# Scan's filler products cut into pieces of two contraction tiles, two of them moved between the six mask products

## The chip, the cores and the metric

The kernel runs on one core of one Trainium2 chip. The metric is the device time of one execution in microseconds (us); lower is better. Engines are called PE (TensorE matmul), PEld (TensorE weight load), DVE (VectorE), ACT (ScalarE), POOL (GpSimd) and SP (SyncE, which issues the DMAs).

## The reference, cut to what matters

Two layers of a backbone over 512 latent tokens and 256 context tokens. Each layer projects the modulated input `h` by one wide weight `w_in` (queries, keys, values, Fourier channels, gates, recurrent channels), runs three branches on parts of that projection, merges them, and ends in a convolutional feed-forward block. One branch is a bidirectional recurrence (8 heads of 64 channels, two directions); the first layer needs its outputs for all tokens, the last layer for the context tokens needs the final state alone.

```python
def _in_proj(h, w_in, names=None):
    out, off = {}, 0
    for name, width in IN_GROUPS:
        if names is None or name in names:
            out[name] = h @ w_in[:, off:off + width]
        off += width
    return out

def _wkv_scan(decay, kd, v, kk, b, s0, r=None):
    ...
    def step(s, inp):
        w_t, k_t, v_t, kk_t, b_t = inp[:5]
        sk = jnp.einsum('dbhvk,dbhk->dbhv', s, kk_t)
        s = s * w_t[..., None, :] - sk[..., None] * b_t[..., None, :] + v_t[..., None] * k_t[..., None, :]
        y = jnp.einsum('dbhvk,dbhk->dbhv', s, inp[5]) if len(inp) == 6 else None
        return s, y
```

## The kernel before, in words

The change lies in `rwkv_scan`, which runs once per layer. It computes the recurrence in blocks: a group `g` is 128 tokens of each direction `d` (two chunks of 64), and a layer has six groups, two of context tokens and four of latent ones. A group is a chain of small steps, PE product, then DVE or ACT on the result, then the next PE product. While PE would wait for the other engines it works on something else: the products of the wide input projection that the recurrence does not need (value, query, key, Fourier and gate channels). These are the filler products, issued by `fill(point, g)` (matmuls of L893).

The work of `fill` is planned ahead. There are 52 slots (128 output channels each, one 512 KB weight block); a slot is one piece for the 512 latent tokens and, where context tokens are needed too, one for the 256 context tokens. A piece is eight contraction tiles of 128 (`KT` = 8), accumulated in one PSUM bank, and each contraction tile is three fp32r matmuls (high and low halves of the operands): 512 or 256 columns wide. Pieces are cut into parts (L736): before, a 512-wide piece is two parts of four contraction tiles, a 256-wide piece is one part of eight, so a part is 12 matmuls 512 wide or 24 matmuls 256 wide. The list `wanted` says at which point of a group a part stands, in the order in which points get their share, and `points` is the order in which they come in the program. Each finished piece is copied from PSUM by ACT (L1119), split and stored; ACT walks the same points in `copy_pieces`.

The first step of a direction is the one that the change touches. PE computes four or six masked products, 16 matmuls of 64x64 each (L916), in this order: NAT and T (banks 0 and 1), MT and, where outputs are wanted, QB (banks 2 and 3), then QK where outputs are wanted and TT (banks 4 and 5). DVE multiplies each by a mask on its way to SBUF (L1267 NAT, L1268 T, L1270 MT, L1272 QB, L1274 QK, L1276 TT). DVE starts NAT when the second product is done, MT when the fourth is done and QK when the last is done. PE then transposes four operands (L937) into banks 0 to 3, and for that waits until all masks are done (semaphore `prod`), since the banks are reused. Before, `fill("prod0" or "prod1", g)` stands between the last product and the transposes, with one part. Behind the transposes stands `fill("turn0" or "turn1", g)`, which has a part in the first layer and none in the last. The second direction's products first wait for ACT's copies of the first one's transposes. Then come five levels of a triangular inverse for both directions (L945 to L1002, L1291 to L1305), and the state steps (L1015 to L1100), each with its fill points.

In the first layer all six groups want outputs: 12 directions of six products. In the last layer the two context groups don't: 4 directions of four products and 8 of six. A direction is named below by the time at which its first product starts.

Of the kernel before, what the change touches and what calls it, by code (L numbers as in the profile page):

```python
# [32 lines left out]
KT = D_MODEL // P  # L33
# [101 lines left out]
def program(nc, A, out):  # L135
    with ExitStack() as top:
# [314 lines left out]
        BOTH = ((0, SEQ), (SEQ, CTX_LEN))  # L451
# [235 lines left out]
        def rwkv_scan(l, s2, h, rings, o_w, last, late):  # L687
# [13 lines left out]
            Kttm, NAT, T, TT, Y, MT = ([spare[:, (2 * i + d) * GCOL:(2 * i + d + 1) * GCOL] for d in range(2)] for i in range(6))  # L701
# [31 lines left out]
            ends = [sum(p <= s for p, _ in pieces) for s in range(len(slots))]  # L733
            parts = []
            for i, (s, w) in enumerate(pieces):
                parts += [(i, s, w, range(0, 4)), (i, s, w, range(4, 8))] if w == BOTH[0] else [(i, s, w, range(8))]  # L736

            points = ["prod0", "turn0", "prod1", "turn1"] + [f"{k}{n}" for n in range(5) for k in ("Y", "offT")]
            points += ["W1", "W2", "U0", "S0", "U1", "S1", "end"]
            wanted = ["prod0", "prod1", "W1", "W2", "U0", "S0", "U1", "S1"] + [f"Y{n}" for n in range(5)] + [f"offT{n}" for n in range(5)]  # L740
            wanted += ["end", "turn1", "turn0"] + [f"offT{n}" for n in range(5)] + ["W1", "prod0", "prod1"]
            n_first = 8
            share = [(len(parts) - n_first) * (g + 1) // N_G - (len(parts) - n_first) * g // N_G for g in range(N_G)]
            span, first = {("first", 0): (0, n_first)}, n_first
            for g in range(N_G):
# [23 lines left out]
            with stage(nc) as (block, sem):  # L769
# [109 lines left out]
                def _(pe):  # L879
# [19 lines left out]
                    for g in range(N_G):  # L899
                        want_y, R = want[g], rI[g % 2]  # L900
                        for d in range(2):

                            pe.wait_ge(sem("fm"), before(n_fm, g, d) + n_fm[g])
                            if d:
                                pe.wait_ge(sem("tm"), 8 * g + 4)
                            elif g:
                                pe.wait_ge(sem("S"), 2 * g)
                                if want[g - 1]:
                                    pe.wait_ge(sem("YR"), y_before(g))
                                    pe.wait_ge(sem("Ysum"), y_before(g))  # L910

                            def product(b, o, stat, mov, turned_rows=False):
                                for t in range(CTILES):
                                    for i in range(2):
                                        for hh in range(2):
                                            m = pe.matmul(ps[rows(row_of(hh, t, i) if turned_rows else i), (b + hh) * 512 + o + t * C:(b + hh) * 512 + o + (t + 1) * C],  # L916
                                                          stat[rows(hh), tc(t, i):tc(t, i) + C], mov[rows(hh), tc(t, i):tc(t, i) + C],
                                                          start=True, stop=True)
                                m.then_inc(sem("pmm"), 1)

                            product(0, 0, Bh[d], Kt[d], True)
                            product(0, 256, Kt[d], Bh[d], True)
                            product(2, 0, EN[d], Kt[d])
                            if want_y:
                                product(2, 256, Bh[d], R[d])
                            if d:
                                pe.wait_ge(sem("prod"), before(n_pr, g, d))
                            if want_y:
                                product(4, 0, EN[d], R[d])
                            product(4, 256, Bh[d], Kt[d])  # L930
                            fill(f"prod{d}", g)

                            pe.wait_ge(sem(f"v{d}"), 16 * (g + 1))
                            pe.wait_ge(sem("prod"), before(n_pr, g, d) + n_pr[g])
                            for b, src in ((0, Kt[d]), (1, Bp[d]), (2, Lr[d]), (3, vI[d])):
                                for t in range(CTILES):
                                    m = pe.transpose(bank(b, P, t * P), src[:, t * P:(t + 1) * P], ident[:, :])  # L937
                                m.then_inc(sem("tmm"), 1)
                            fill(f"turn{d}", g)
# [168 lines left out]
                def _(act):  # L1108
# [44 lines left out]
                        act.wait_ge(sem("exp"), n + 3)  # L1153
                        act.activation(L[:, :], L[:, :], ACT.Exp, scale=-DECAY).then_inc(sem("exp"), 1)

                    copy_pieces(0, "first", some=slice(0, 2))
                    decays(0, 0)
                    copy_pieces(0, "first", some=slice(2, 6))
                    decays(0, 1)
                    copy_pieces(0, "first", some=slice(6, n_first))  # L1160
                    for g in range(N_G):
                        for d in range(2):
                            for n_tm, (b, dst) in enumerate(((0, Kttm), (1, Btm), (2, Ktm), (3, Vtm))):
                                act.wait_ge(sem("tmm"), 8 * g + 4 * d + n_tm + 1)
                                act.activation(dst[d][:, :], bank(b), ACT.Copy).then_inc(sem("tm"), 1)
                            copy_pieces(g, f"prod{d}", f"turn{d}")
                        for n_lv in range(5):
                            for d in range(2):
                                act.wait_ge(sem(f"Ymm{d}"), 5 * g + n_lv + 1)
# [1344 lines left out]
```

## Time and profile before

| | |
|---|---|
| runs of the kernel before, median of 3 | 3658.41 us (3656.13 to 3660.78) |
| span of the profiled execution | 3653.4 us, 5.0 us below that median |
| PE busy | 3375.0 us (92%) |
| PEld busy | 2696.8 us (74%) |
| DVE busy | 1582.8 us (43%) |
| ACT, POOL busy | 1268.5 us (35%), 1071.4 us (29%) |
| PE matmul and weight-load instructions | 36725 each |
| mean granted TensorE clock | 0.971 |
| scan of the first layer, of the last layer | about 255 to 880 us, about 2270 to 2800 us |

Times in rows count from the span's start. The span is from the first to the last instruction of one execution; a run's time holds it and what lies around it, so the times of the runs are a few us longer.

### The profile page before, as it was taken

The page shows a single profiled execution, that of the slowest core. Times are in us where ns is not written, and L with a number is a line of the kernel's source. Part 1 is how long each engine was busy: PE and PEld are TensorE (multiplying, and loading weights), DVE is VectorE, ACT ScalarE, POOL GpSimd, SP SyncE. Part 2 cuts the span into 40 slices and gives each one's busy share as a digit, 9 for nine tenths or more (in the row PEclk, how much of TensorE's full clock was granted, in tenths as well). Part 3 has the DMA queues.
Part 4 walks back from the last instruction along what each step waited for, and adds up shares of the span by engine and source line. Part 5 has one row for each costly group of instructions (what it writes and reads, how often), then busy time and mean ns, then how long its engine had stood idle before and what let it go on. Part 6 is the DMA issues. An engine that isn't in the chain of part 4 may idle for free. (4 is left out here: it accounts for less than half of the span.)

```text
span 3653.4 us, 82760 instructions
## 1 busy us (share of the span) xinstructions
PE 3375.0 (92%) x36725; PEld 2696.8 (74%) x36725; DVE 1582.8 (43%) x2538; ACT 1268.5 (35%) x2184; POOL 1071.4 (29%) x645
## 2 busy tenths in 40 slices
PE   6989999999888999799999899999899898889998
PEld 4668888888655777687878676887778666568887
DVE  3243334442377546512112734445453476372224
ACT  3333233333365412321212243334344465233222
POOL 1111133233011412332333132223333114235553
PEclk8999999999999999999999999999999999989999
DMA  7664333443212343233332145344343313423332
GB/s 260 213 204 113 111 113 90 119 121 96 83 58 96 102 140 104 81 116 121 116 116 94 50 142 182 101 113 128 115 128 92 104 58 121 165 84 104 98 98 87
DMA packets 444861, 423.43 MB, mean 116 GB/s; under 512 B 15652, under 2 KB 372042, under 8 KB 437594
## 3 DMA queue, kind: packets, MB, share of 16 engines
q1 hardware_dynamic: 442922, 409.35, 35.7%
q10 hardware_dynamic: 1584, 8.78, 0.6%
q8 instruction: 291, 4.77, 0.5%
q14 instruction: 64, 0.52, 0.0%
HBM read 329.34 MB, written 88.74 MB: 114 GB/s over the span
## 5 line engine op out<-in xcount | busy, mean ns | idle before, releaser
L893 PE MATMUL ps<-I-321_h_hi,I-324_w_hi 128*128 128x256 f32 (+1 forms) x832 | 294.8, 354 | 4.5 <-PEq L124 4.5
L893 PE MATMUL ps<-I-322_h_lo,I-324_w_hi 128*128 128x256 f32 (+1 forms) x832 | 282.0, 339 | 0.0
L893 PE MATMUL ps<-I-321_h_hi,I-325_w_lo 128*128 128x256 f32 (+1 forms) x832 | 281.8, 339 | 0.0
L2372 POOL TENSOR_TENSOR I-18800_w_lo<-I-18798_w_raw,I-18799_w_hi 128x1024 fp32r<-128x1024 f32 x60 | 145.1, 2418 | 342.6 <-ACT I-18799_w_hi L2335 342.5
L893 PE MATMUL ps<-I-23550_h_hi,I-23553_w_hi 128*128 128x512 f32 (+1 forms) x544 | 212.7, 391 | 4.6 <-PEq L124 4.6
L893 PE MATMUL ps<-I-23551_h_lo,I-23553_w_hi 128*128 128x512 f32 (+1 forms) x544 | 200.9, 369 | 0.0
L893 PE MATMUL ps<-I-23550_h_hi,I-23554_w_lo 128*128 128x512 f32 (+1 forms) x544 | 200.6, 369 | 0.0
L2372 POOL TENSOR_TENSOR I-39040_w_lo<-I-39038_w_raw,I-39039_w_hi 128x1024 fp32r<-128x1024 f32 x60 | 144.5, 2408 | 154.6 <-ACT I-39039_w_hi L2335 154.6
L2335 ACT ACTIVATE I-18799_w_hi<-I-18798_w_raw 128x1024 fp32r<-128x1024 f32 x61 | 64.6, 1059 | 355.0 <-PE ps L370 235.3
L370 PE MATMUL ps<-I-18795_h_hi,I-18799_w_hi 128*128 128x512 f32 x704 | 182.8, 341 | 1.1 <-DVE I-18796_h_lo L407 1.1
L370 PE MATMUL ps<-I-18795_h_hi,I-18800_w_lo 128*128 128x512 f32 x704 | 182.6, 340 | 0.0
L370 PE MATMUL ps<-I-18796_h_lo,I-18799_w_hi 128*128 128x512 f32 x704 | 180.1, 337 | 0.0
L893 PEld LDWEIGHTS ps<-I-321_h_hi,I-324_w_hi 128*128 128x128 f32 x832 | 158.5, 191 | 25.4 <-issue 4.9
L857 POOL TENSOR_TENSOR I-325_w_lo<-I-323_w_raw,I-324_w_hi 128x1024 fp32r<-128x1024 f32 x34 | 81.9, 2408 | 320.1 <-ACT I-324_w_hi L1137 320.1
L893 PEld LDWEIGHTS ps<-I-321_h_hi,I-325_w_lo 128*128 128x128 f32 x832 | 158.5, 191 | 17.2
L893 PEld LDWEIGHTS ps<-I-322_h_lo,I-324_w_hi 128*128 128x128 f32 x832 | 158.8, 191 | 14.6
L1119 ACT ACTIVATE I-1999_result<-ps 128x512 f32<-128x512 f32 x104 | 51.3, 493 | 327.7 <-PE ps L893 327.5
L857 POOL TENSOR_TENSOR I-23554_w_lo<-I-23552_w_raw,I-23553_w_hi 128x1024 fp32r<-128x1024 f32 x34 | 83.7, 2462 | 275.7 <-ACT I-23553_w_hi L1137 275.7
L963 PE MATMUL ps<-I-49_x 64*64 64x32 f32 x3840 | 149.3, 220 | 1.4 <-issue 1.4
L370 PE MATMUL ps<-I-39035_h_hi,I-39039_w_hi 128*128 128x512 f32 x352 | 137.9, 392 | 1.1 <-DVE I-39036_h_lo L407 1.1
L370 PE MATMUL ps<-I-39036_h_lo,I-39039_w_hi 128*128 128x512 f32 x352 | 137.1, 389 | 0.0
L370 PE MATMUL ps<-I-39035_h_hi,I-39040_w_lo 128*128 128x512 f32 x352 | 137.0, 389 | 0.0
(902 smaller groups left out, 8757.7 us busy)
## 6 DMA issues: line engine op xcount, KB each, us to landing
I-323_w_raw<-in_w_in SPq DMA_DIRECT2D x67, 512.0 KB, 5.8
I-23552_w_raw<-in_w_in SPq DMA_DIRECT2D x67, 512.0 KB, 5.2
I-18808_ada_w<-in_ada_w SPq DMA_DIRECT2D x24, 1024.0 KB, 6.0
I-18798_w_raw<-in_ffn_up SPq DMA_DIRECT2D x44, 512.0 KB, 3.8
I-39038_w_raw<-in_ffn_up SPq DMA_DIRECT2D x44, 512.0 KB, 3.8
proj_d<-I-1999_result SPq DMA_DIRECT2D x52, 384.0 KB, 3.0
I-507_ada_w<-in_ada_w SPq DMA_DIRECT2D x16, 1024.0 KB, 5.8
I-18798_w_raw<-in_ffn_down SPq DMA_DIRECT2D x22, 512.0 KB, 3.3
```

Of the source, the lines that this page charges most:

```text
L370: m = pe.matmul(dst[:, at:at + n], w[wi][:, k, :], a[ai][:, k, at:at + n], start=k == 0 and i == 0, stop=k == kt - 1 and i == 2)
L857: pool.tensor_tensor(lo(s), raw(s), hi(s).bitcast(F32), ALU.subtract).then_inc(sem("w_lo"), 1)
L893: m = pe.matmul(bank(6 + i % 2, n_c), w[:, k, :], hv[:, k, c0:c0 + n_c], start=k == 0 and v == 0, stop=k == KT - 1 and v == 2)
L963: return pe.matmul(side(ps[rows(i), (2 + d) * 512 + c0:(2 + d) * 512 + c0 + C], n_lv, 1 - d), Y[d][rows(i), c0:c0 + C], side(TT[d][rows(i) ...
L1119: act.activation(res[:, s % 2, c0:c0 + n_c], bank(6 + i % 2, n_c), ACT.Copy, scale=DH_A ** -0.5 if J_Q <= slots[s][0] < J_K else 1.0).then ...
L2335: act.activation(pair(g)[0], rings[0][:, g % 3, :, :], ACT.Copy).then_inc(sem("w_hi"), 1)
L2372: pool.tensor_tensor(pair(g)[1], rings[0][:, g % 3, :, :], pair(g)[0].bitcast(F32), ALU.subtract).then_inc(sem("w_lo"), 1)
```

## The change

A part is halved: two contraction tiles of a 512-wide piece, four of a 256-wide one (6 or 12 matmuls). The number of parts doubles, every entry of `wanted` stands twice, and the first 16 half parts instead of the first 8 parts stand ahead of the first group. In place of one part at `prod0` and `prod1`, one half part stands at a new point, `early0` or `early1`, behind the second product, and one at `prod0` or `prod1`, behind the fourth where outputs are wanted; where they are not, that half part stays behind the last product. ACT's copies follow the same points.

```diff
-                parts += [(i, s, w, range(0, 4)), (i, s, w, range(4, 8))] if w == BOTH[0] else [(i, s, w, range(8))]
-
-            points = ["prod0", "turn0", "prod1", "turn1"] + [f"{k}{n}" for n in range(5) for k in ("Y", "offT")]
+                n_k = 2 if w == BOTH[0] else 4
+                parts += [(i, s, w, range(k, k + n_k)) for k in range(0, KT, n_k)]
+
+            points = ["early0", "prod0", "turn0", "early1", "prod1", "turn1"] + [f"{k}{n}" for n in range(5) for k in ("Y", "offT")]
...
-            n_first = 8
+            whole = ["W1", "W2", "U0", "S0", "U1", "S1"] + [f"Y{n}" for n in range(5)] + [f"offT{n}" for n in range(5)]
+            whole += ["end", "turn1", "turn0"] + [f"offT{n}" for n in range(5)] + ["W1", "prod0", "prod1"]
+            wanted = ["early0", "prod0", "early1", "prod1"] + [p for p in whole for _ in range(2)]
+            n_first = 16
...
                             product(0, 0, Bh[d], Kt[d], True)
                             product(0, 256, Kt[d], Bh[d], True)
+                            fill(f"early{d}", g)
                             product(2, 0, EN[d], Kt[d])
                             if want_y:
                                 product(2, 256, Bh[d], R[d])
+                                fill(f"prod{d}", g)
                             if d:
                                 pe.wait_ge(sem("prod"), before(n_pr, g, d))
                             if want_y:
                                 product(4, 0, EN[d], R[d])
                             product(4, 256, Bh[d], Kt[d])
-                            fill(f"prod{d}", g)
+                            if not want_y:
+                                fill(f"prod{d}", g)
```

On PE, the first direction of the last group of the last layer before (the first row is the last filler matmul ahead of it; `kk_in` and `EN` hold scaled keys, `Bh` and `r_in` the other operands, `ident` is the identity of the transposes; the filler rows left out repeat the three shown):

```order
L893 MATMUL ps<-I-23550_h_hi,I-23554_w_lo 128x512
L916 MATMUL ps<-I-24941_kk_in,I-24931_Bh 64x64 x16
L916 MATMUL ps<-I-24931_Bh,I-24941_kk_in 64x64 x16
L916 MATMUL ps<-I-24941_kk_in,I-24927_EN 64x64 x16
L916 MATMUL ps<-I-24945_r_in,I-24931_Bh 64x64 x16
L916 MATMUL ps<-I-24945_r_in,I-24927_EN 64x64 x16
L916 MATMUL ps<-I-24941_kk_in,I-24931_Bh 64x64 x16
L893 MATMUL ps<-I-23550_h_hi,I-23553_w_hi 128x512
L893 MATMUL ps<-I-23551_h_lo,I-23553_w_hi 128x512
L893 MATMUL ps<-I-23550_h_hi,I-23554_w_lo 128x512
...
L937 MATMUL ps<-I-50_ident,I-24941_kk_in 128x128 x4
```

The same place on PE after the change, with the new line numbers:

```order
L918 MATMUL ps<-I-24941_kk_in,I-24931_Bh 64x64 x16
L918 MATMUL ps<-I-24931_Bh,I-24941_kk_in 64x64 x16
L895 MATMUL ps<-I-23550_h_hi,I-23553_w_hi 128x512
...
L918 MATMUL ps<-I-24941_kk_in,I-24927_EN 64x64 x16
L918 MATMUL ps<-I-24945_r_in,I-24931_Bh 64x64 x16
L895 MATMUL ps<-I-23550_h_hi,I-23553_w_hi 128x512
...
L918 MATMUL ps<-I-24945_r_in,I-24927_EN 64x64 x16
L918 MATMUL ps<-I-24941_kk_in,I-24931_Bh 64x64 x16
L942 MATMUL ps<-I-50_ident,I-24941_kk_in 128x128 x4
```

The twelve filler matmuls that stood between the sixth product and the transposes stand in two lots of six, behind the second and the fourth product, and the transposes follow the sixth product directly.

On PE, the first direction of the last layer's first context group before, four products and 24 filler matmuls 256 wide, and then after the change:

```order
L916 MATMUL ps<-I-24941_kk_in,I-24931_Bh 64x64 x16
L916 MATMUL ps<-I-24931_Bh,I-24941_kk_in 64x64 x16
L916 MATMUL ps<-I-24941_kk_in,I-24927_EN 64x64 x16
L916 MATMUL ps<-I-24941_kk_in,I-24931_Bh 64x64 x16
L893 MATMUL ps<-I-23550_h_hi,I-23553_w_hi 128x256
...
L937 MATMUL ps<-I-50_ident,I-24941_kk_in 128x128 x4
```

```order
L918 MATMUL ps<-I-24941_kk_in,I-24931_Bh 64x64 x16
L918 MATMUL ps<-I-24931_Bh,I-24941_kk_in 64x64 x16
L895 MATMUL ps<-I-23550_h_hi,I-23553_w_hi 128x256
...
L918 MATMUL ps<-I-24941_kk_in,I-24927_EN 64x64 x16
L918 MATMUL ps<-I-24941_kk_in,I-24931_Bh 64x64 x16
L895 MATMUL ps<-I-23550_h_hi,I-23553_w_hi 128x256
...
L942 MATMUL ps<-I-50_ident,I-24941_kk_in 128x128 x4
```

Here half of the filler matmuls, twelve, moved ahead of the third product, and twelve stay ahead of the transposes. On ACT, DVE, POOL and SP no instruction changes its place. Over a group the number of filler matmuls is the same to within one half part.

## Rows read from the trace of the kernel before

**Rows 1.** PE's waits (line waited for: us in total, times, longest us), first layer's scan.

```profile
PE ps L916 <- issue: 18.2, 12, 3.4
PE ps L1068 <- DVE I-49_x L1339: 6.7, 3, 4.8
```

**Rows 2.** The same view, last layer's scan.

```profile
PE ps L916 <- issue: 8.6, 6, 1.8
PE ps L958 <- DVE I-49_x L1291: 6.3, 4, 4.3
```

**Rows 3.** Timeline (start us, us, engine line op) of the direction that starts at 730.46.

```profile
730.14 0.39 PE L893 MATMUL ps<-I-321_h_hi,I-325_w_lo 128*128 128x512 f32 x1
730.46 0.69 PE L916 MATMUL ps<-I-1991_kk_in,I-1981_Bh 64*64 64x64 f32 x32
...
730.95 1.29 POOL L866 TENSOR_TENSOR I-1999_result<-I-1999_result,I-2000_rope 128x512 f32<-128x512 f32 x1
...
731.69 0.69 DVE L1267 TENSOR_TENSOR I-49_x<-ps,I-1954_masks 128x512 f32<-128x512 f32 x1 [3.35 <-PE ps L916]
...
734.29 0.45 PE L916 MATMUL ps<-I-1991_kk_in,I-1981_Bh 64*64 64x64 f32 x14 [0.93 <-issue]
...
734.67 0.50 PE L893 MATMUL ps<-I-321_h_hi,I-324_w_hi 128*128 128x512 f32 x1
...
734.79 0.69 DVE L1274 TENSOR_TENSOR I-1971_QK<-ps,I-1954_masks 128x512 f32<-128x512 f32 x1 [0.62 <-PE ps L916]
735.01 0.39 PE L893 MATMUL ps<-I-322_h_lo,I-324_w_hi 128*128 128x512 f32 x1
...
735.40 0.68 DVE L1276 TENSOR_TENSOR I-49_x<-ps,I-1954_masks 128x512 f32<-128x512 f32 x1
...
737.53 0.60 PE L937 MATMUL ps<-I-50_ident,I-1991_kk_in 128*128 128x128 f32 x4
```

**Rows 4.** DMA queues (packets, MB, share of 16 engines): whole span, then 731.8 to 732.9.

```profile
q8 instruction: 291, 4.77, 0.5%
...
q8 instruction: 1, 0.02, 5.6%
```

**Rows 5.** Windows (columns in the first row), first product to first transpose, 19 directions.

```profile
core 0: us, PE busy (x) PEld busy (x) DVE busy (x) ACT busy (x) POOL busy (x), PEclk, DMA share, GB/s
...
391.19:402.34 11.15, 7.74 (x205) 6.54 (x205) 5.07 (x8) 0.00 (x0) 1.85 (x1) 0.85 0.38 106
...
2473.37:2479.30 5.93, 5.93 (x216) 5.86 (x217) 4.67 (x8) 2.70 (x5) 0.00 (x0) 1.00 0.01 3
...
2769.91:2775.74 5.83, 5.83 (x205) 5.21 (x205) 4.56 (x8) 0.00 (x0) 0.00 (x0) 1.00 0.02 5
...
sum 147.06, PE 121.24 PEld 107.85 DVE 97.37 ACT 25.95 POOL 50.25; mean PE 6.38 PEld 5.68 DVE 5.12 ACT 1.37 POOL 2.64
```

**Rows 6.** Timeline of the first direction of the first layer, its last mask and transposes.

```profile
273.40 0.68 DVE L1276 TENSOR_TENSOR I-49_x<-ps,I-1954_masks 128x512 f32<-128x512 f32 x1
...
274.23 0.63 PE L937 MATMUL ps<-I-50_ident,I-1991_kk_in 128*128 128x128 f32 x4 [1.33 <-DVE I-49_x L1276]
```

**Rows 7.** Windows: stretches in and behind idle stretches of PE, columns as in rows 5.

```profile
281.63:283.63 2.00, 0.01 (x1) 0.00 (x0) 0.93 (x2) 0.00 (x0) 0.00 (x0) 1.00 0.00 0
858.83:861.98 3.15, 0.00 (x1) 0.00 (x0) 0.69 (x2) 0.00 (x0) 2.79 (x3) 1.00 0.42 120
862.60:866.00 3.40, 3.40 (x10) 2.63 (x9) 2.33 (x4) 0.00 (x0) 0.00 (x0) 0.50 0.00 0
...
2566.34:2568.07 1.73, 0.00 (x0) 0.00 (x0) 0.69 (x2) 1.30 (x3) 0.27 (x1) 1.00 0.18 46
2569.20:2572.60 3.40, 3.40 (x9) 2.55 (x9) 3.33 (x3) 0.00 (x0) 3.40 (x3) 0.50 0.22 65
...
276.30:279.70 3.40, 3.40 (x68) 2.67 (x70) 0.00 (x0) 1.87 (x4) 1.38 (x1) 1.00 0.46 127
```

**Rows 8.** DMA queues, 856.7 to 859.4 us.

```profile
q1 hardware_dynamic: 1439, 0.72, 99.9%
```

More of the change, by code:

```diff
@@ L735, in rwkv_scan @@
             for i, (s, w) in enumerate(pieces):
-                parts += [(i, s, w, range(0, 4)), (i, s, w, range(4, 8))] if w == BOTH[0] else [(i, s, w, range(8))]
-            points = ["prod0", "turn0", "prod1", "turn1"] + [f"{k}{n}" for n in range(5) for k in ("Y", "offT")]
+                n_k = 2 if w == BOTH[0] else 4
+                parts += [(i, s, w, range(k, k + n_k)) for k in range(0, KT, n_k)]
+            points = ["early0", "prod0", "turn0", "early1", "prod1", "turn1"] + [f"{k}{n}" for n in range(5) for k in ("Y", "offT")]
             points += ["W1", "W2", "U0", "S0", "U1", "S1", "end"]
-            wanted = ["prod0", "prod1", "W1", "W2", "U0", "S0", "U1", "S1"] + [f"Y{n}" for n in range(5)] + [f"offT{n}" for n in range(5)]
-            wanted += ["end", "turn1", "turn0"] + [f"offT{n}" for n in range(5)] + ["W1", "prod0", "prod1"]
-            n_first = 8
+            whole = ["W1", "W2", "U0", "S0", "U1", "S1"] + [f"Y{n}" for n in range(5)] + [f"offT{n}" for n in range(5)]
+            whole += ["end", "turn1", "turn0"] + [f"offT{n}" for n in range(5)] + ["W1", "prod0", "prod1"]
+            wanted = ["early0", "prod0", "early1", "prod1"] + [p for p in whole for _ in range(2)]
+            n_first = 16
             share = [(len(parts) - n_first) * (g + 1) // N_G - (len(parts) - n_first) * g // N_G for g in range(N_G)]
@@ L1154, in decays @@
                         act.activation(L[:, :], L[:, :], ACT.Exp, scale=-DECAY).then_inc(sem("exp"), 1)
-                    copy_pieces(0, "first", some=slice(0, 2))
+                    copy_pieces(0, "first", some=slice(0, 4))
                     decays(0, 0)
-                    copy_pieces(0, "first", some=slice(2, 6))
+                    copy_pieces(0, "first", some=slice(4, 12))
                     decays(0, 1)
-                    copy_pieces(0, "first", some=slice(6, n_first))
+                    copy_pieces(0, "first", some=slice(12, n_first))
                     for g in range(N_G):
@@ L1165, in _ @@
                                 act.activation(dst[d][:, :], bank(b), ACT.Copy).then_inc(sem("tm"), 1)
-                            copy_pieces(g, f"prod{d}", f"turn{d}")
+                            copy_pieces(g, f"early{d}", f"prod{d}", f"turn{d}")
                         for n_lv in range(5):
```

## Prediction

> **What bounds the kernel now.** I read the waits of PE first, since PE is busy for 92% of the span. In the scans the largest entry is "L916 <- issue", 18.2 us in 12 waits in the first layer and 8.6 us in 6 in the last [rows 1, 2]: "issue" means that PE waits for nothing that another engine does. The timeline of one direction shows where. PE runs through five masked products and half of the sixth without a break, stands for 0.93 us with 14 of the sixth's 32 rows to go, and goes on [rows 3]. The DMA view has an instruction queue that carries 291 packets, 4.77 MB; with 73,450 matmuls and weight loads on PE in the table above that is one packet of 16 KB for about 256 PE instructions, and in this direction one of them stands alone in the window ahead of the break [rows 4]. I read the break as PE out of instructions: six products are 384 of them (192 matmul rows, 192 loads) and pass in 2.8 us, faster than the next packet comes. The windows view then prices it. From first product to first transpose a direction takes 5.83 us without a break (a 256-wide filler part: 5.93 us), and up to 11.15 us with one; 19 of the 20 six-product directions together take 147.06 us [rows 5]. The reader is to see that this stretch is a pure PE chain: DVE and ACT are waited for nowhere in it. The twentieth is the very first direction, where DVE is late and ends the wait [rows 6].
>
> The second thing in these windows is the clock. Behind a break of 3.15 us and behind one of 1.73 us the granted clock is 0.50, the 1.2 GHz level, for about 3.4 us; in a break of 2.00 us, and in the window of the direction that holds it, it is 1.00 [rows 7].
>
> **What the change removes.** The base without breaks is 15 x 5.83 + 4 x 5.93 = 111.2 us, so breaks and slow clock cost 147.06 - 111.2 = 35.9 us in these 19 directions. With filler matmuls behind the second and the fourth product, the 256 records between two packets no longer pass in 1.9 us. The break with 14 rows to go puts the packet boundary ahead of it into the second product (192 - 14 = 178 rows, with the loads 356 instructions, less 256: the 100th, and a product has 64); to the next boundary PE then has two lots of fillers, about 2 x 1.3 us, and most of the four other products, together about 4.5 to 5 us. From a boundary to the resumption it takes the 1.9 us that 256 product instructions need, plus the break: 1.9 + 0.93 + 0.22 = 3.1 us in the direction shown, and some 5.3 us where data traffic holds the packet up (the break of 3.15 us, with the data queue at 99.9% just before it, [rows 7, 8]). So I take all of the 35.9 us as saved, less 0.7 us that the two late packets may still cost.
>
> **What it adds.** All new durations are in one direction's rows [rows 3]. The first filler matmul starts 0.15 us behind the last product matmul (which starts at 734.29 + 0.45 - 0.22 = 734.52), the second 0.34 us behind the first, the others 0.229 us apart (735.01 to 737.53 is 11 steps), and from the last filler matmul to a product it is 0.32 us (730.14 to 730.46). Half a part is 0.34 + 4 x 0.229 = 1.26 us from first to last. The six products alone are 5.83 - 2.86 - 0.15 = 2.82 us, in three pairs 2.79 us. So from first product to last product matmul: 2.79 + 2 x (0.15 + 1.26 + 0.32) = 6.25 us.
>
> Then comes the wait that the filler part used to hide. QK and TT can be masked only when the last product is done, and the transposes wait for TT. QK starts 734.79 - 734.52 = 0.27 us behind the last product matmul, TT 0.61 us later [rows 3], and the transposes 0.83 us behind TT's start (273.40 to 274.23, [rows 6]): 1.71 us with no cover. In the kernel before the same 1.71 us lay under 2.86 us of filler. A direction becomes 6.25 + 1.71 = 7.96 us, 2.13 us over the unbroken 5.83 us; a 256-wide one shifts by the same. 19 x 2.13 = 40.5 us.
>
> The bounds of the 1.71 us: not under 1.4 us (two masks at 0.60 us and the two hand-overs cannot overlap), and not much over it, unless POOL slows the masks; with POOL busy beside it (730.95 to 732.24) the mask at 731.69 took 0.69 us as elsewhere [rows 3], so I take 1.71. What is queued behind the waiting transposes on PE is the turn filler, the second direction and the five levels; nobody else waits meanwhile, since ACT only copies transposes.
>
> The four-product directions had no break and keep half a part ahead of the transposes, 1.6 us, which hides the one late mask. They pay the extra switch alone: 0.15 + 0.32 us, less 0.11 us as one filler step falls away, 0.35 us each, 1.4 us in all. The first direction of all stays bound by DVE: zero. The doubled lists move filler work by at most half a part at other points and cost nothing where the pieces end as before; no other engine's order changes.
>
> **The sum.** -35.9 + 0.7 + 40.5 + 1.4 = +6.7 us: 3653.4 + 6.7 = 3660.1 us of span. The runs' median lies 5.0 us over the span, so 3665 us, +0.18%. In words: the break in the instruction stream goes, and a wait for DVE of the same size takes its place.
>
> The Trainium skill's page "Runtime: NRT & Kernel Launch", section "Instruction fetch mechanics", describes the refills in blocks of 256 instructions and says of a crossing that it is "mostly hidden". The trace disagrees for these products: 18 breaks, 26.8 us together [rows 1, 2]. By the page nothing would be saved and the sum would be near +42 us, which is the first rival.
>
> **Rivals.** First, slower: the breaks stay, because a packet is asked for only after PE has gone some way into the block and the wait for DVE then holds up the asking. For it: the packet came some 2 us later where data traffic was thick [rows 8]. Against it: the boundary falls into the second product, and 2.6 us of filler now lie behind it. If all stayed, the 35.9 us would not be saved: about 3700 us. From a fifth of them on (7 us) it decides between no difference and slower.
>
> Second, slower: the clock. Each direction now has PE idle for about 1.5 us (1.71 less the last matmul's 0.22) with only short matmuls and transposes around it. A break of 1.73 us was followed by the lower level, one of 2.00 us shows no such thing [rows 7]. A slow stretch of 3.4 us at half speed costs at most 1.7 us; I take 1.5 us each time. If a third of 19 waits do it, +9.5 us, 3674.5 us; all of them, 3693 us. The Trainium skill's page "TensorE: Matmul & The Clock Gate", Part 4, says that transposes do not count as PE being busy; by that the idle stretch would be longer than the 1.5 us and the falls likely. The trace does not bear it out: behind the first direction's wait of 1.33 us [rows 6] and its transposes the window from 276.30 us shows the granted clock at 1.00 [rows 7].
>
> Third, faster: the waits for DVE elsewhere, 6.7 us at the state step [rows 1] and 6.3 us at the levels [rows 2], with one slow-clock stretch behind each of the longest two. DVE is late there with preparing the next group, whose loads and POOL's splits follow the filler pieces. Where the filler stream is shifted by half a part, these start about 1.4 us earlier. If all vanished: 13 us and some 6 us of clock, 3665 - 19 = 3646 us. It decides when 14 of the 19 us go. Against it: one part more or less early is 1.4 us, and the two longest waits are 4.8 and 4.3 us.
>
> That the change doesn't do what it says is excluded: the new order has the fillers between the products.
>
> **How the numbers follow.** A difference under 0.2%, 7.3 us, can't be told from none in this kernel. My forecast has a chance of 0.66, with 3658 to 3673 us as its own range; the clock 0.18, the breaks 0.07, the faster waits 0.09. The predicted time is the forecast's. The range of 8 in 10 takes in the clock's third and leaves its far end and the breaks: 3656 to 3678 us. Faster by over 0.2%: 0.08, from the third rival. Slower by over 0.2%: most of the first two (0.21) and a third of the forecast (0.21), 0.42. Same: 0.50.
>
> **What would show it.** In the new profile the waits "L918 <- issue" should fall from 26.8 us to a few us, and a wait of the transposes for DVE's TT (L942) should appear, about 1.5 us each, some 28 us in about 20 waits. The windows from first product to first transpose should all be near 8.0 us. The half-clock stretches behind the products, at 863 and 2569 us in the old trace, should be gone. I am wrong if the transposes' wait is much shorter than 1.5 us, if issue waits stay above 10 us, or if the lower clock level appears behind the new waits.

## The result and the profile after

The changed kernel takes 3668.53 us (median of 10 runs, 3662.38 to 3676.89), the kernel before took 3655.75 us beside it (10 runs, 3651.27 to 3664.23). The ratio is 1.0035, with a 95% interval of 1.0024 to 1.0046: slower by some 13 us, and more than the 0.2% that can be told from none. The forecast was 3665 us.

PE's waits in the first layer's scan come first, as in [rows 1] (line waited for: us in total, times, longest us). In the changed kernel the products are at L918, the fillers at L895, the transposes at L942. The view begins at 160 us; its entries for PEq and ada_row lie ahead of the scan.

```profile
PE ps L942 <- DVE I-49_x L1281: 18.0, 12, 1.5
PE ps L1073 <- DVE I-49_x L1344: 5.7, 3, 4.8
PE ps L895 <- PEq L124: 4.5, 1, 4.5
PE ps L198 <- ACT I-66_ada_row L189: 2.5, 1, 2.5
PE ps L895 <- ACT I-2001_turned L1131: 2.4, 1, 2.4
PE ps L963 <- DVE I-49_x L1296: 0.2, 1, 0.2
```

The same view of the last layer's scan, against [rows 2]:

```profile
PE ps L942 <- DVE I-49_x L1281: 12.0, 8, 1.5
PE ps L963 <- DVE I-49_x L1296: 6.5, 3, 4.3
...
PE ps L968 <- DVE I-49_x L1296: 1.8, 1, 1.8
```

"L918 <- issue" is in neither list: all 26.8 us of breaks in the instruction stream are gone. In their place stand 20 waits of the transposes for DVE, 30.0 us. The waits for DVE at the state step (9.4 us over both scans in either kernel) and at the levels (7.2 against 6.9 us) are nearly what they were. Two entries are new that I had not forecast: fillers that wait for ACT's rotated copies (2.4 us), and a level step that waits 1.8 us for DVE.

The timeline shows one six-product direction as it now runs (one of the kernel before stands in [rows 3]): two products, half a part, two products, half a part, two products, then an empty PE.

```profile
631.97 0.65 PE L918 MATMUL ps<-I-1982_Bh,I-1992_kk_in 64*64 64x64 f32 x32
...
632.55 0.50 PE L895 MATMUL ps<-I-321_h_hi,I-324_w_hi 128*128 128x512 f32 x1
...
637.33 0.65 PE L918 MATMUL ps<-I-1992_kk_in,I-1982_Bh 64*64 64x64 f32 x32
...
638.04 0.69 DVE L1279 TENSOR_TENSOR I-1972_QK<-ps,I-1954_masks 128x512 f32<-128x512 f32 x1 [1.39 <-PE ps L918]
638.65 0.68 DVE L1281 TENSOR_TENSOR I-49_x<-ps,I-1954_masks 128x512 f32<-128x512 f32 x1
...
639.48 0.63 PE L942 MATMUL ps<-I-50_ident,I-1992_kk_in 128*128 128x128 f32 x4 [1.50 <-DVE I-49_x L1281]
```

The windows from first product to first transpose of the same 19 directions as in [rows 5], and the two stretches behind such a wait:

```profile
core 0: us, PE busy (x) PEld busy (x) DVE busy (x) ACT busy (x) POOL busy (x), PEclk, DMA share, GB/s
394.95:403.01 8.06, 6.56 (x211) 5.63 (x211) 3.97 (x7) 0.00 (x0) 1.83 (x1) 1.00 0.54 148
...
2482.42:2490.51 8.09, 6.59 (x216) 6.08 (x217) 3.97 (x7) 2.71 (x5) 0.00 (x0) 1.00 0.02 4
...
2787.25:2795.28 8.03, 6.53 (x206) 5.20 (x205) 3.98 (x7) 0.00 (x0) 0.00 (x0) 1.00 0.01 2
...
sum 152.99, PE 124.48 PEld 102.96 DVE 75.53 ACT 22.48 POOL 52.00; mean PE 6.55 PEld 5.42 DVE 3.98 ACT 1.18 POOL 2.74
```

```profile
639.48:642.90 3.42, 3.42 (x24) 3.12 (x25) 1.71 (x2) 2.07 (x4) 0.56 (x1) 1.00 0.02 7
...
2479.55:2482.95 3.40, 2.46 (x50) 2.26 (x54) 1.27 (x2) 2.71 (x6) 0.12 (x1) 1.00 0.00 0
```

The reader is to see that the spread is gone. Before, a direction took anything from 5.83 to 11.15 us; now 18 of the 19 take 8.02 to 8.09 us and one takes 8.25. The sum rises by 152.99 - 147.06 = 5.9 us. The four-product directions take 0.35 to 0.42 us more each, 1.5 us in all, and the first direction 0.7 us less: +6.8 us with rounding. In both stretches behind a wait the clock is at 1.00. In the two scans of this trace it falls four times, each time in or right behind a longer wait (4.8, 2.4, 4.3 and 1.8 us), and never behind one of the 20 waits of 1.5 us.

That is half of the 13 us. Two places in the same scans, outside the first steps, cost another 3.9 and 4.8 us, so 15.5 us are named. The traces scatter by more than what this is off: the span of this one is 21.5 us longer than the one before (3675.0 against 3653.4 us), that of a second trace of the change (below) 9.1 us, with 15.8 us in the same items. So the three items stand in both traces, but how they divide the median's 13 us is not shown.

The first place is in the first layer's fifth group. From the first direction's transposes to the second direction's first product it takes 8.61 us (741.44 to 750.05) against 4.71 before. The timeline of the changed kernel there, then a window (columns as above):

```profile
744.03 0.63 ACT L1124 ACTIVATE I-1999_result<-ps 128x512 f32<-128x512 f32 x1
...
744.68 2.39 ACT L1131 ACTIVATE I-2001_turned<-ps 32x512 f32<-32x512 f32 x4
747.10 0.38 ACT L1124 ACTIVATE I-1999_result<-ps 128x256 f32<-128x256 f32 x1
747.22 0.77 PE L895 MATMUL ps<-I-321_h_hi,I-324_w_hi 128*128 128x512 f32 x1 [2.42 <-ACT I-2001_turned L1131]
```

```profile
746.80:750.20 3.40, 2.98 (x10) 2.00 (x14) 0.00 (x0) 1.69 (x4) 1.54 (x2) 0.50 0.55 202
```

A half part here begins a new piece, in the bank of the piece before the last. ACT empties that bank in five instructions, and only after four copies for the transposes. Of the 3.9 us, 2.4 are the wait; the rest comes with the clock, which is at 0.50, the lower level, behind it.

The second place is in the last layer's fifth group, from the second direction's transposes to the next group: 87.67 against 82.89 us, with 6.8 us at half clock (2747.0 to 2753.8). The two windows, before and after:

```profile
2687.02:2769.91 82.89, 80.84 (x1717) 67.57 (x1716) 36.34 (x70) 35.43 (x77) 32.64 (x20) 1.00 0.49 145
...
2699.58:2787.25 87.67, 82.40 (x1710) 68.77 (x1710) 43.22 (x72) 36.00 (x77) 32.74 (x20) 0.96 0.48 137
```

PE stands idle for 5.3 us in place of 2.1, 3.2 us more, and is busy for 1.6 us more, although half a part less of filler (six matmuls, some 1.4 us) falls into the stretch. So the slow clock costs about 3 us there.

### The profile page after: what moved, and what is told of

It is laid out like the page before. It is cut to its first block and busy times, and to the rows that moved or that the text cites. A ratio compares the mean times of both kernels' runs of the same rounds, so it can differ in the third digit from the quotient of the medians.

```text
span 3675.0 us, 82760 instructions
## 1 busy us (share of the span) xinstructions
PE 3392.7 (92%) x36725; PEld 2700.1 (73%) x36725; DVE 1589.3 (43%) x2538; ACT 1270.0 (35%) x2184; POOL 1068.3 (29%) x645
## 5 line engine op out<-in xcount | busy, mean ns | idle before, releaser
L895 PE MATMUL ps<-I-321_h_hi,I-324_w_hi 128*128 128x256 f32 (+1 forms) x832 | 296.3, 356 | 7.0 <-PEq L124 4.5
L895 PE MATMUL ps<-I-322_h_lo,I-324_w_hi 128*128 128x256 f32 (+1 forms) x832 | 281.8, 339 | 0.0
L895 PE MATMUL ps<-I-321_h_hi,I-325_w_lo 128*128 128x256 f32 (+1 forms) x832 | 281.6, 338 | 0.0
L895 PE MATMUL ps<-I-23550_h_hi,I-23553_w_hi 128*128 128x512 f32 (+1 forms) x544 | 214.2, 394 | 4.6 <-PEq L124 4.6
L895 PE MATMUL ps<-I-23551_h_lo,I-23553_w_hi 128*128 128x512 f32 (+1 forms) x544 | 200.9, 369 | 0.0
L895 PE MATMUL ps<-I-23550_h_hi,I-23554_w_lo 128*128 128x512 f32 (+1 forms) x544 | 200.8, 369 | 0.0
L895 PEld LDWEIGHTS ps<-I-321_h_hi,I-324_w_hi 128*128 128x128 f32 x832 | 158.2, 190 | 28.8 <-issue 8.0
L895 PEld LDWEIGHTS ps<-I-321_h_hi,I-325_w_lo 128*128 128x128 f32 x832 | 158.3, 190 | 17.5
L895 PEld LDWEIGHTS ps<-I-322_h_lo,I-324_w_hi 128*128 128x128 f32 x832 | 158.7, 191 | 14.1
L968 PEld LDWEIGHTS ps<-I-49_x 64*64 64x64 f32 x3840 | 132.4, 136 | 6.7 <-issue 6.4
```

The lines of the kernel that those rows point to most:

```text
L895: m = pe.matmul(bank(6 + i % 2, n_c), w[:, k, :], hv[:, k, c0:c0 + n_c], start=k == 0 and v == 0, stop=k == KT - 1 and v == 2)
L968: return pe.matmul(side(ps[rows(i), (2 + d) * 512 + c0:(2 + d) * 512 + c0 + C], n_lv, 1 - d), Y[d][rows(i), c0:c0 + C], side(TT[d][rows(i) ...
```

## The experiments

In all of them "one half early" means a six-product direction with one half part among its products and the other behind the last.

**The halves back behind the last product.** Parts halved as in the change, both half parts behind the last product.

```diff
-                            fill(f"early{d}", g)
                             product(2, 0, EN[d], Kt[d])
...
                             product(4, 256, Bh[d], Kt[d])
+                            fill(f"early{d}", g)
+                            fill(f"prod{d}", g)
```

> The parts are halved as in the change, but both halves of a direction stay behind its last product. Theory (the breaks in the instruction stream depend on the six products running in one piece; a separate cost of some 4 to 8 us comes from groups that get an odd number of half parts): the breaks return, some 20 to 30 us of issue waits, first product to first transpose is as before, and only the shift costs: about 3656 + 6 = 3662 us, ratio 1.001 to 1.002. Rival (halving costs nothing, the whole 12.8 us are the new place of the fillers): ratio 1.000. Rival (halving alone makes the breaks go): no issue waits at this line, and a gain near 30 us.

Ratio 1.0006 (0.9992 to 1.0020). "L918 <- issue" is back, 19.7 us in the first layer and 8.3 us in the last. Halving alone removes no break; the new places do. A cost of the odd groups is within this interval, but not shown by it. Both places are in its trace: at the first it has the same wait of 2.4 us for ACT's rotated copies, but no slow clock, 7.28 us in place of 4.71; at the second it takes 4.8 us more than before.

**Even groups.** The changed kernel, but each group is given an even number of half parts, so that outside the first steps every point holds what it held before.

```diff
-share = [(len(parts) - n_first) * (g + 1) // N_G - (len(parts) - n_first) * g // N_G for g in range(N_G)]
+share = [2 * ((len(parts) - n_first) // 2 * (g + 1) // N_G - (len(parts) - n_first) // 2 * g // N_G) for g in range(N_G)]
```

> The changed kernel, but each group is given an even number of half parts, so that outside the first steps every filler point holds what it held before. Theory (two costs: about 6.8 us from the first steps, the rest from the odd shift): the filler's wait for ACT's rotated copies behind the transposes goes, and the time is 3656 + 7 = 3663 us, ratio 1.0015 to 1.0025. Rival (the rest is not the shift, but the new place of the first steps' fillers, or chance): ratio stays at 1.0035.

Ratio 1.0018 (1.0006 to 1.0029), 6.6 us; in its trace the first steps cost 6.5 us. All 20 waits of 1.5 us are there, the wait for the rotated copies is gone, and the first place takes 4.74 us again. The second still takes 2.4 us more than before, with the clock at 1.00. The intervals of this ratio and of the change's overlap a little: the trace settles the 3.9 us of the first place, not the rest.

**The changed kernel again**, for a second trace.

> The changed kernel once more, for a second trace. The two places outside the first steps where it lost time, +3.9 us behind the first direction of the first layer's fifth group and +4.8 us behind the last layer's fifth group, the second with a half-clock stretch of 6.8 us. Theory: the first one comes back, since its wait for the rotated copies is set by the order of the parts; the second may not, since a kernel with the same odd groups showed 1.2 us there and one with even groups 5.1 us. Rival (both belong to the odd shift): both come back.

Both places come back, +3.90 and +4.72 us; the run took 3664.45 us. So neither is chance. But the second is in the trace of every kernel with halved parts, from +1.2 to +4.8 us with odd groups and from +2.4 to +5.1 us with even ones, so it is not the odd shift that sets it; the kernels with whole parts and moved packet borders have -0.6 to +1.8 us there. The timeline of this second trace shows DVE's preparation of the next group beside POOL's work:

```profile
2728.84 1.30 POOL L868 TENSOR_TENSOR I-24949_result<-I-24949_result,I-24950_rope 128x512 f32<-128x512 f32 x1 [2.46 <-DMA proj_d<-I-24949_result]
...
2730.21 1.63 POOL L871 TENSOR_TENSOR I-24951_turned<-I-24951_turned,I-24949_result 128x512 f32<-128x512 f32 x1
2730.60 1.78 DVE L1239 TENSOR_TENSOR I-24931_Bh<-I-24929_a,I-24927_EN 128x512 f32<-128x512 f32 x1
2732.27 2.38 POOL L859 TENSOR_TENSOR I-23554_w_lo<-I-23552_w_raw,I-23553_w_hi 128x1024 fp32r<-128x1024 f32 x1 [0.42 <-ACT I-23553_w_hi L1142]
2732.31 2.88 DVE L1241 TENSOR_TENSOR I-24927_EN<-I-24937_k_in,I-24927_EN 128x512 f32<-128x512 f32 x1
2735.12 0.68 DVE L1243 TENSOR_TENSOR I-24933_Bp<-I-24929_a,I-24925_Lr 128x512 f32<-128x512 f32 x1
```

The same chain in the kernel before, five steps of 0.68 us first, then:

```profile
2727.61 1.77 DVE L1244 TENSOR_TENSOR I-24929_a<-I-24945_r_in,I-24937_k_in 128x512 f32<-128x512 f32 x1
2729.42 1.66 DVE L1246 TENSOR_TENSOR I-24945_r_in<-I-24945_r_in,I-24935_L 128x512 f32<-128x512 f32 x1
```

A step of 0.68 us takes 1.7 to 2.9 us where POOL works beside it. Before, two of POOL's three operations fell on the end of the chain and the third behind it; now all three fall on its first three steps. The chain takes 8.2 us in place of 6.5, the level's copies (L1296) come late, and PE stands. In the changed kernel with even groups all three fall on its last steps, and it takes 8.7 us. POOL's chain follows a store's landing (the first row of the second trace names the DMA of `proj_d`), DVE's follows PE's levels; I read it as their phase that decides which of them meet; no run moved the one against the other alone. The Trainium skill's page "SBUF — State Buffer", section "SBUF: two separate sides", says that a DVE operation with two SBUF inputs and a GpSimd operation that reads SBUF exclude each other for a whole instruction. The trace agrees: these steps stretch, while the masks, which read PSUM, keep their 0.69 us beside POOL (638.04 above, with POOL busy for 1.50 of the window's 1.58 us).

**One half early, behind the second product**, with the change's odd groups, then with even groups.

```diff
                             product(0, 256, Kt[d], Bh[d], True)
                             fill(f"early{d}", g)
...
                             product(4, 256, Bh[d], Kt[d])
-                            if not want_y:
-                                fill(f"prod{d}", g)
+                            fill(f"prod{d}", g)
```

> The changed kernel, but in six-product directions too only the first half part stands early, behind the second product, and the second half stays behind the last product. Theory (breaks go once 256 product instructions take over some 3.2 us; the wait for DVE costs only where no filler covers it): a direction takes about 2.8 + 1.73 + 1.71 = 6.25 us, few breaks remain, the transposes' wait for DVE falls from 1.5 us to some 0.1 us each. 19 directions at 0.4 us over the unbroken 5.83 us are +7.8 us, against 35.9 us saved: with the odd shift some 3656 - 28 + 6 = 3634 us, ratio 0.992 to 0.996. Rival (one half part is too little, the next packet is still late): issue waits of 10 us and more behind the products, ratio 0.998 to 1.003. Rival (the clock falls behind any such change): windows at 0.50 behind the products.

> Both edits: one half part early, one behind the last product, and an even number of half parts for each group. Theory: the gains add, about 3656 - 28 + 1 = 3629 us, ratio 0.990 to 0.994, that is some 6 us under the kernel with one early half alone. Rival (the odd shift costs nothing): the same time as that kernel. Rival (the breaks return with one half part): ratio 0.997 to 1.002.

Ratios 0.9961 (0.9947 to 0.9975) and 0.9952 (0.9935 to 0.9968): both faster than before, by 14 and 18 us. In sign the theory holds, a third of the gain is missing. The two intervals overlap, so the 6 us that I expected between these kernels are not shown. Undisturbed directions take 6.55 us, not 6.25, and breaks of 2.3 and 3.6 us remain in the first layer. The timeline of one direction of the kernel with even groups (transposes at L940):

```profile
725.54 0.65 PE L918 MATMUL ps<-I-1993_r_in,I-1977_EN 64*64 64x64 f32 x32
725.79 0.69 DVE L1273 TENSOR_TENSOR I-49_x<-ps,I-1954_masks 128x512 f32<-128x512 f32 x1 [1.39 <-PE ps L918]
726.01 0.65 PE L918 MATMUL ps<-I-1991_kk_in,I-1981_Bh 64*64 64x64 f32 x32
726.40 0.68 DVE L1275 TENSOR_TENSOR I-1969_QB<-ps,I-1954_masks 128x512 f32<-128x512 f32 x1
...
727.00 0.68 DVE L1277 TENSOR_TENSOR I-1971_QK<-ps,I-1954_masks 128x512 f32<-128x512 f32 x1
...
727.60 0.68 DVE L1279 TENSOR_TENSOR I-49_x<-ps,I-1954_masks 128x512 f32<-128x512 f32 x1
...
728.42 0.41 PE L940 MATMUL ps<-I-50_ident,I-1991_kk_in 128*128 128x128 f32 x2 [0.18 <-DVE I-49_x L1279]
```

Four masks run in one chain, 0.61 us apart, from the end of the fourth product; TT is late by that chain, not by the sixth product.

**One half early, behind the fourth product**, even groups.

```diff
-                            fill(f"early{d}", g)
...
                                 product(2, 256, Bh[d], R[d])
+                            fill(f"early{d}", g)
```

> As the kernel with one early half part and even groups, but the early half stands behind the fourth product instead of the second. In that kernel an unbroken direction took 6.55 us, 0.29 us more than the six products, the two half parts and the 1.71 us wait give, because DVE masks four pairs in a chain that starts only after the fourth product. Theory: with the half part behind the fourth product two of the four masks run beside it, QK can start right behind the sixth product, and a direction takes 6.26 us: some 14 x 0.29 = 4 us less than with the half behind the second, ratio to before 0.992 to 0.996. Rival (the first four products in one piece outrun the instruction packets again): breaks of over 10 us in the issue waits, ratio 0.996 to 0.999. Rival (the 0.29 us are not DVE's chain): same time as with the half behind the second.

Ratio 0.9951 (0.9937 to 0.9965): the same as behind the second. An undisturbed direction does take 6.28 us, so the chain of masks was the 0.27 us. But the 19 directions together gain only 1.1 us by it (128.4 against 129.5 us). Nine of them are undisturbed, against twelve with the half behind the second product; the breaks at the products are 3.4 us in the first layer (3.6 there) and 2.4 us in the last (1.0 there).

**The whole part behind the fourth product**, even groups: the change without its split.

> The changed kernel with even groups, but both half parts of a six-product direction stand together behind the fourth product. Theory: one switch between products and fillers less than in the change (0.15 + 0.32 us, less 0.11 us), the same bare wait for DVE: a direction takes 8.02 - 0.36 = 7.66 us, 20 of them some 7 us less than the even version of the change, about 3656 to 3659 us, ratio 0.999 to 1.001, if no breaks return; the transposes' wait stays 1.5 us each. Rival (the first four products run into the packets' end): breaks of 5 to 15 us more. Rival (the added time is not the bare wait but the splitting): a gain of 20 us and more.

Ratio 1.0008 (0.9997 to 1.0020). An undisturbed direction takes 7.64 us, 0.38 less than in the change, with 20 waits for DVE (18.5 us in the first layer, below, and 12.0 in the last) and one break of 0.6 us at the products.

```profile
PE ps L943 <- DVE I-49_x L1282: 18.5, 12, 2.0
```

So the second switch costs 0.38 us a direction, and the bare wait is the main price.

**Packet borders moved.** The kernel before, with 32 small matmul calls ahead of each scan. Each call is two matmul rows and two loads in the trace, so each lot is 128 instructions, not the 64 that I had counted.

```diff
+                    for _ in range(32):
+                        pe.matmul(ps[0:C, 0:C], ident[0:C, 0:C], ident[0:C, 0:C], start=True, stop=True)
                     fill("first", 0)
```

> The kernel before with 32 small matmuls (32 rows and their 32 weight loads, 64 instructions) ahead of each scan; their results are overwritten. Theory (the breaks stand where a packet of 256 PE instructions ends): the breaks of the first layer move by 32 matmul rows, from 14 rows to go in the sixth product to 46 rows to go, that is into the fifth product (or the directions that had none get one); the total of the issue waits may change, the time within 10 us. Rival (the breaks have to do with the place in the direction, a bank, a semaphore or a load, not with the count of instructions): the breaks stay at 14 rows to go.

Ratio 0.9979 (0.9968 to 0.9990). In the first layer, 128 instructions on, the waits at L918 fall from 18.2 to 0.3 us. In the last layer, 256 instructions on, 9.9 us remain, at the rows where they stood before. That is what a border every 256 instructions, 128 rows, would do: in the direction of [rows 3], PE runs from a border at row 50 to one at row 178 in 1.9 us; with the border at row 114 alone, fillers lie ahead of it. The 12 windows of the first layer lose 23.9 us. The window of the fourth direction, 11.15 us in [rows 5], and PE's waits at the products, first layer, then last:

```profile
392.60:398.42 5.82, 5.82 (x206) 5.20 (x206) 4.56 (x8) 0.00 (x0) 1.85 (x1) 1.00 0.73 203
```

```profile
PE ps L918 <- issue: 0.3, 1, 0.3
...
PE ps L918 <- issue: 9.9, 7, 2.1
```

Yet only 8 us are left of it: the added rows made the scan start 5.6 us late, and between the scans, where the borders had moved as well, the trace is 7.3 us longer. That the moved borders cost these 7.3 us is not shown: PE has no wait "<- issue" between the scans in either trace, and the kernel with half the shift (below), whose borders there are moved by the same 128 instructions, is 1.7 us longer than before.

**Borders moved in the first layer only**, 32 narrow calls, put back ahead of its last transposes; then the same with one half early in the last layer.

```diff
+                    for _ in range(0 if last else 32):
+                        pe.matmul(ps[0:C, 0:4], ident[0:C, 0:C], ident[0:C, 0:4], start=True, stop=True)
                     fill("first", 0)
...
                             pe.wait_ge(sem("prod"), before(n_pr, g, d) + n_pr[g])
+                            for _ in range(32 if not last and g == N_G - 1 and d else 0):
+                                pe.matmul(ps[0:C, 0:4], ident[0:C, 0:C], ident[0:C, 0:4], start=True, stop=True)
```

> The kernel before, its own fillers and order, with 32 narrow matmul calls (64 matmul rows and 64 loads, 128 instructions) ahead of the first layer's scan and again ahead of its very last transposes, so that every other stage keeps its packet borders; their results are overwritten. Theory (a direction breaks when two packet borders, 128 rows apart, both fall into its 192 product rows; 128 instructions move them from rows 50 and 178 to row 114 alone): no breaks in the first layer's directions, the last layer's at the same rows as before. The first shifted kernel won 24 us in these windows, lost 5.6 us to wide pads and some 7 us between the scans, where its borders had moved too; here only about 2 us of pads remain: 3657 - 22 = 3635 us, ratio 0.993 to 0.996. Rival (what the breaks cost is lost elsewhere as soon as they go): ratio 0.997 to 0.999, as the first shifted kernel's.

> The same pads, and in the last layer the six-product directions with one half part behind the second product and one behind the last; halved parts, even groups. Theory: on top of the aligned kernel the last layer's directions save about 5 us as in the kernel with one half early: ratio 0.991 to 0.995. Rival (halved parts move DVE's preparation against POOL's work in the last layer, a loss of 3 to 5 us behind its fifth group): no faster than the aligned kernel.

Ratios 0.9963 (0.9951 to 0.9976) and 0.9950 (0.9934 to 0.9965). At the products of the first layer 0.3 us of breaks are left at most, but the pads, as I call the added rows, cost much of what the breaks gave back. The two intervals overlap: a further gain from the half part early in the last layer is not shown by these times. The scan starts 9.3 us late:

```profile
243.20 3.97 PE L899 MATMUL ps<-I-50_ident 64*64 64x4 f32 x36 [4.54 <-PEq L124]
...
854.19 3.89 PE L938 MATMUL ps<-I-50_ident 64*64 64x4 f32 x64
```

```profile
234.70:255.20 20.50, 15.96 (x84) 12.81 (x85) 6.26 (x11) 0.00 (x0) 0.52 (x1) 0.50 0.73 214
```

Rows of 4 columns on one and the same quarter of the array take 0.11 us each at the lower clock and 0.06 at the higher (first fence, timeline). That is no less than the first shift's rows of 64 columns, which took 7.1 us for 64 at the lower clock. The half-clock stretch about the start of the scan is 20.5 us long (second fence, a window), 6.8 to 13.7 us in all the other traces.

**Half that shift**: the first of these two with 16 calls, 64 instructions.

> As the aligned kernel, but with 16 calls instead of 32, 64 instructions. Theory (borders of 256 instructions): the first layer's borders move by 32 rows, from rows 50 and 178 of a direction to about 18 and 146, so the breaks come back, each 32 rows earlier than in the kernel before (143, 145, 132, 156 instead of 175, 177, 164, 188), with issue waits near 18 us in the first layer. Rival (any shift breaks the pattern): no breaks, or breaks at unchanged rows.

One run, 3649.64 us. The breaks come back where the count puts them: in the ninth direction with 14 rows to go in the fifth product, not in the sixth [rows 3]. So do all six breaks of over 0.2 us in the first layer: each stands 32 rows earlier than in the kernel before.

```profile
726.93 0.52 PE L918 MATMUL ps<-I-1993_r_in,I-1977_EN 64*64 64x64 f32 x18
728.08 0.40 PE L918 MATMUL ps<-I-1993_r_in,I-1977_EN 64*64 64x64 f32 x12 [0.63 <-issue]
```

The total is smaller than I expected, 7.7 us against some 18. The first border now lies nearer to the fillers; that the fetch runs ahead of PE there would explain it, but no run tests this.

**Pads moved**: the shift by 128 with one half early in the last layer, its first pads behind the first direction's masks, 32 columns wide and in the products' own order, which alternates between quarters.

```diff
+                            for n in range(32 if not last and (g, d) in ((0, 0), (N_G - 1, 1)) else 0):
+                                i, hh = n // 2 % 2, n % 2
+                                pe.matmul(ps[rows(i), hh * 512:hh * 512 + 32], ident[rows(hh), 0:C], ident[rows(hh), 0:32], start=True, stop=True)
```

> As the aligned mix, but the first pads stand ahead of the transposes of the very first direction, which is not bound by PE's products, instead of ahead of the scan, and both pads are 32 calls of the products' own form, which alternate between the halves of the array. In the aligned kernels the pads ran 0.11 us a row ahead of the scan, on a stretch of half clock that grew from 6.8 to 20.5 us, and made it start 9.3 us late; at the end they took 3.9 us. Theory: at the products' 15 ns a row both pads cost some 1 us each, the breaks stay away, and the time is the aligned mix's less 9.3 - 1 and 3.9 - 1 us: about 3660 - 18 - 11 = 3631 us, ratio 0.990 to 0.993. Rival (the late start of the scan was not the pads' doing): the same ratio as the aligned mix, 0.995.

Ratio 0.9930 (0.9916 to 0.9944), 3633.57 us: 24 us under the kernel before. The pads cost 1.1 and 1.2 us (timeline of the first); place and form of the pads changed together, so the run doesn't say which of the two did it. A direction that held 5.3 us of break and slow clock [rows 5] takes 5.82 us (window).

```profile
273.22 1.14 PE L943 MATMUL ps<-I-50_ident 64*64 64x32 f32 x64 [0.37 <-DVE I-49_x L1285]
```

```profile
388.18:394.00 5.82, 5.82 (x206) 5.20 (x206) 4.56 (x8) 0.00 (x0) 1.84 (x1) 1.00 0.73 203
```

## Why the prediction was right, and where it was not

**The breaks go.** Right: 35.9 us of breaks and slow clock, forecast as saved but for 0.7, are gone from these windows entirely. The reading behind it, a border every 256 instructions, is now shown by the shifts: 64 instructions moved six breaks by 32 rows each, 128 took out the first layer's, 256 left the last layer's at their rows. From the row 128 rows ahead of a break to the resumption, which the prediction put at 3.1 and some 5.3 us, it is 2.8 to 3.5 us in nine of the first layer's directions and 4.1 to 5.6 us in three. The "mostly hidden" of the Trainium skill's page "Runtime: NRT & Kernel Launch", section "Instruction fetch mechanics", stays contradicted.

**The bare wait.** Right: 7.96 us a direction were forecast and 8.02 to 8.09 measured; waits of 1.5 us in 20 places were forecast with 28 us in all, and 30.0 measured. The sum over the first steps was +6.7 us against +6.8 measured here, and 6.5 us in the trace of the kernel with even groups. The four-product directions cost 0.35 to 0.42 us each (0.35 forecast); the very first direction, put at zero, gained 0.7 us.

**The clock.** The second rival fell: none of the 20 waits is followed by the lower level, with transposes right behind each, as the first direction's row had said [rows 7]. By the Trainium skill's page "TensorE: Matmul & The Clock Gate", Part 4, as the prediction read it, a fall was likely; no row here shows it. The clock did fall at one place that the prediction had not seen: behind the 2.4 us wait for the rotated copies, in both traces of the change. The kernel with both halves last has that wait without the fall and takes 1.3 us less there.

**"The doubled lists move filler work by at most half a part at other points and cost nothing where the pieces end as before."** This step failed. Where a group gets an odd number of half parts, the pieces do not end as before: one begins before ACT has emptied its bank, 3.9 us at one place in both traces and none with even groups. The time came out only 3.5 us over the forecast, in its range, but in part by luck: the sum starts from 3653.4 + 5.0 = 3658.4 us, and the kernel before took 3655.75 us beside the change. The added time is 12.8 us where 6.7 was forecast, and "same", which had the larger chance (0.50 against 0.42 for slower), is not what was measured.

**The faster rival.** The waits at L1068 and L958 [rows 1, 2] stayed at 4.8 and 4.3 us. Its idea, that the phase of the stream to DVE's preparation matters, fits what the traces show, with the other sign: a new wait of 1.8 us and a slow clock at one place, 4.7 to 4.8 us in both traces of the change.

Left open: what sets the phase of POOL's work to DVE's chain at the second place, and why the half shift left smaller breaks.

## What to carry to other kernels

A stall "<- issue" in a run of small matmuls is cheaper to move than to fill: count the instructions between packet borders, and shift the stream at a place where the engine waits anyway, by as many as bring one border instead of two into the run (128 here; 64 left 7.7 us of breaks). Work that separates products may also be what hides the wait behind them: before it is moved, ask what the next instruction waits for, and leave half of it there. When a list of pieces is made finer, keep every old border where it was.

## What the hardware showed that was not expected

- 128 instructions more, and nothing else changed, took 18 us of breaks out of the first layer. A change that adds or removes instructions ahead of such a stretch can gain or lose that much without touching it.
- With 64 narrow rows ahead of the scan TensorE ran at the lower level (1.2 GHz) for 20.5 us, in both kernels that had them; without, for 6.8 to 13.7 us.
- DVE's steps between SBUF tiles went from 0.68 to as much as 2.88 us beside POOL, while masks that read PSUM stayed at 0.69 us.
